# Two-block transformer, attention: ScalarE makes the new pair's exponentials before it copies the transposed pair

## What is computed

```python
s = jnp.einsum('bthd,btkd->bthk', qi, k_sel) * HEAD_DIM ** -0.5
p = masked_softmax(s, valid[:, :, None, :]).astype(v.dtype)
return jnp.einsum('bthk,btkd->bthd', p, v_sel)
```

```python
o = gi[..., 0:1] * o_c + gi[..., 1:2] * o_s + gi[..., 2:3] * o_w
```

```python
s = jnp.einsum('bshd,bnhd->bhsn', q, k).astype(jnp.float32) * HEAD_DIM ** -0.5
p = jax.nn.softmax(s, axis=-1).astype(v.dtype)
return jnp.einsum('bhsn,bnhd->bshd', p, v).reshape(B, S, MEM_Q)
```

## Time and profile before

| what | value |
|---|---|
| median of three runs | 3473.38 us |
| the profiled execution | 3475.57 us |
| its span (first to last instruction) | 3473.8 us |
| its mean granted TensorE clock | 0.966 |
| busy: PE, weight loads, VectorE, ScalarE, GpSimd | 94, 77, 46, 41, 46% of the span |

### The profile page before, as it was taken

How to read it: one execution, slowest core, us unless ns; L and a number is a source line. 1 busy time by engine, 2 the same in 40 slices (tenths; PEclk the granted TensorE clock), 3 DMA queues, 4 the chain that set the end, 5 groups by cost and what they waited for, 6 DMA issues and landing times.

```text
span 3473.8 us, 45512 instructions
## 1 busy us (share of the span) xinstructions
PE 3272.7 (94%) x16902; PEld 2669.8 (77%) x16902; DVE 1596.8 (46%) x2361; ACT 1438.5 (41%) x2575; POOL 1597.1 (46%) x1404
## 2 busy tenths in 40 slices
PE   6789999998999999999988996999999999999998
PEld 4567888876568888788877775888888888888886
DVE  4783443142743431444247875555565562234421
ACT  3355333223764333333235554454454532243332
POOL 4245445652555446444553321444444434464454
PEclk8899999997999999999999997999999999999999
DMA  4111333341013333333332120111111113333332
GB/s 121 45 43 55 97 97 95 94 116 37 1 32 96 96 95 95 91 97 95 96 82 60 51 61 25 31 38 42 38 37 37 41 46 99 98 95 97 97 96 68
DMA packets 471306, 245.86 MB, mean 71 GB/s; under 512 B 13819, under 2 KB 468710, under 8 KB 471014
## 3 DMA queue, kind: packets, MB, share of 16 engines
q1 hardware_dynamic: 470144, 241.33, 24.5%
q10 hardware_dynamic: 998, 2.30, 0.2%
HBM read 241.51 MB, written 2.10 MB: 70 GB/s over the span
## 4 chain that ended last, share of the span: by engine, by line
PE 84%; DVE 9%; ACT 4%; issue 2%; POOL 1%; DMA 0%; ACTq 0%; DVEq 0%; POOLq 0%
PE ps L464 18%; PE ps L466 18%; PE ps L465 18%; PE ps L2207 2%; PE ps L2311 2%; PE ps L2208 2%; PE ps L2209 2%; PE ps L1538 2%; PE ps L2293 2%; PE ps L1548 2%; PE ps L1561 1%; PE ps L1726 1%; PE ps L1799 1%; PE ps L1727 1%; PE ps L1728 1%
## 5 line engine op out<-in xcount | busy, mean ns | idle before, releaser
L446 POOL TENSOR_TENSOR w_lo<-ring,w_hi 128x512 fp32r<-128x512 f32 (+1 forms) x908 | 1222.7, 1368 | 1542.9 <-ACT w_hi L437 1542.9
L437 ACT ACTIVATE w_hi<-ring 128x512 fp32r<-128x512 f32 (+1 forms) x908 | 516.0, 617 | 1269.4 <-PE ps L466 1189.5
L464 PE MATMUL ps<-h_hi,w_hi 128*128 128x512 f32 x1776 | 702.7, 396 | 4.6 <-POOL w_lo L446 4.4
L466 PE MATMUL ps<-h_hi,w_lo 128*128 128x512 f32 x1776 | 693.4, 390 | 0.0
L465 PE MATMUL ps<-h_lo,w_hi 128*128 128x512 f32 x1640 | 640.1, 390 | 0.0
L464 PEld LDWEIGHTS ps<-h_hi,w_hi 128*128 128x128 f32 x1776 | 334.4, 188 | 81.1 <-POOL w_lo L446 6.4
L466 PEld LDWEIGHTS ps<-h_hi,w_lo 128*128 128x128 f32 x1776 | 334.1, 188 | 69.8
L465 PEld LDWEIGHTS ps<-h_lo,w_hi 128*128 128x128 f32 x1640 | 308.8, 188 | 68.2 <-issue 4.8
L465 PE MATMUL ps<-a_lo,w_hi 128*128 128x512 f32 x752 | 292.9, 390 | 0.0
L466 PE MATMUL ps<-a_hi,w_lo 128*128 128x512 f32 x720 | 280.4, 390 | 0.0
L464 PE MATMUL ps<-a_hi,w_hi 128*128 128x512 f32 x720 | 280.4, 389 | 0.0
(11 more groups left out here) (446 smaller groups left out, 5809.7 us busy)
## 6 DMA issues: line engine op xcount, KB each, us to landing
ring<-in_ffn_w_in SPq DMA_DIRECT2D x176, 512.0 KB, 3.8
ring<-in_w_in SPq DMA_DIRECT2D x96, 512.0 KB, 4.0
ring<-in_ffn_w_down SPq DMA_DIRECT2D x32, 512.0 KB, 4.1
ring<-in_ffn_w_out SPq DMA_DIRECT2D x32, 512.0 KB, 3.8
ring<-in_w_o SPq DMA_DIRECT2D x16, 512.0 KB, 4.1
ring<-in_w_branch_gdn SPq DMA_DIRECT2D x16, 512.0 KB, 3.8
ring<-in_nsa_w_in SPq DMA_DIRECT2D x15, 512.0 KB, 3.9
ring<-in_dsa_w_in SPq DMA_DIRECT2D x13, 512.0 KB, 4.1
```

What stands on the lines that cost most here:

```text
L437: act.activation(w_hi[:, (halves(u) + j) % PIECES, 0:n, :], slot(u)[:, j * n:(j + 1) * n, :], ACT.Copy) \
L446: pool.tensor_tensor(w_lo[:, q % PIECES, 0:n, :], slot(u)[:, j * n:(j + 1) * n, :], w_hi[:, q % PIECES, 0:n, :].bitcast(f32), ALU.subtract ...
L464: pe.matmul(dst, wh, hi(k), start=first and k == 0, stop=False)
L466: ins = pe.matmul(dst, wl, hi(k), start=False, stop=last and k == 2 * n - 1)
```

## The change

In each step of ScalarE's list the exponentials of step i now stand ahead of the copy of step i-3. The instructions, their operands and their semaphores are the same. (The two blocks are exchanged, so the exponentials are now on line 1624 and the copy on line 1634.)

```diff
         for i in range(S + LAG_V + 2):
-            s = i - LAG_T
-            if 0 <= s < S:
-                act.wait_ge(sig("att_turned").sem, t["turned"] + s + 1)
-                if s >= 2:
-                    act.wait_ge(sig("att_value").sem, t["value"] + s - 1)
-                w = min(P, us[2 * s]["nk"])
-                n_t = len(key_tiles(us[2 * s])) * P
-                act.activation(prT4[0:w, 2 * (s % 2):2 * (s % 2) + 2, 0:n_t], ps[0:w, 2:4, 0:n_t], ACT.Copy) \
-                   .then_inc(sig("att_copied").sem, 1)
             if i < S:
                 act.wait_ge(sig("att_max").sem, t["max"] + i + 1)
                 if i >= DEEP:
...
                 ins.then_inc(sig("att_prob").sem, 1)
+            s = i - LAG_T
+            if 0 <= s < S:
+                act.wait_ge(sig("att_turned").sem, t["turned"] + s + 1)
+                if s >= 2:
+                    act.wait_ge(sig("att_value").sem, t["value"] + s - 1)
+                w = min(P, us[2 * s]["nk"])
+                n_t = len(key_tiles(us[2 * s])) * P
+                act.activation(prT4[0:w, 2 * (s % 2):2 * (s % 2) + 2, 0:n_t], ps[0:w, 2:4, 0:n_t], ACT.Copy) \
+                   .then_inc(sig("att_copied").sem, 1)
             e = i - LAG_V - 1
             if pair_end(us, e):
```

## The result

The changed kernel took 3534.8 us, the median of four executions (3529.12 to 3547.99), the profiled one among them; the kernel before had 3473.52 us beside them (four runs, 3468.51 to 3478.00). The ratio is 1.0182, 95% interval 1.0154 to 1.0209: **slower by 61.3 us**. The forecast was 3521, with a range of 3497 to 3560. The profiled execution took 3531.99 us (span 3530.2), 56.4 us above the one before (3475.57). Its four runs (us, mean granted clock) are 3529.12 at 0.964, 3531.99 at 0.961, 3537.61 at 0.959 and 3547.99 at 0.956: the longer the run, the lower the clock.

The account below looks back on a forecast made before the run. The prediction took PE, a row of matmuls holding 84% of the chain of waits, as the bound. Its terms 10.4 + 24.8 + 12.6 = 47.8 us on the median 3473.38 gave 3521 us, range 3497 to 3560.

Parts of the forecast that it names:

- The bound, and what the change does: Both attention stages: PE nearly the bound; copy, transposes and values come behind the maximum, in the loop to scores two steps on.
- Layer 0, 4 x 2.59 = 10.4: Layer 0 attention: a pair takes 12.49 us instead of 9.90, over four full periods, 10.4 us more.
- Layer 1, 5 x 4.95 = 24.8: Layer 1 attention: a pair takes 28.3 us against 23.31, over the five pairs after the first, 24.8 us more.
- Half the sum of the operations, 26.9: Layer 1: lower bound for a pair, half of 53.8 us of operations for each of the even-step and odd-step loops.
- the walk: Layer 1: longest path through a pair's twelve steps, 2.2 + 6.3 + 5.2 + 1.7 + 5.8 + 7.1 = 28.3 us.
- The ends, 12.6: Both layers: memory-head steps 2.9 us, drain 1.2, passage into memory steps 0.4, fill 1.8; twice 6.3, bounds 5 and 16.
- GpSimd stays hidden: Attention stages: GpSimd's normalising comes out one step or more before the new copy, so it adds no time.
- The clock, costed at nothing: Attention stages: PE's layer 0 hole grows to about 2.4 us; holes this size went both ways, so 0 us charged.
- Partial cover: Both stages: loops bind only in the widest steps, PE's slack covers the rest; 24 us more, 3497 us; chance 0.13.
- Gain: Both stages: earlier exponentials start scores sooner and PE loses its waits; some 17 us less, 3456 us; chance 0.04.
- No effect: Both stages: ScalarE is no bound and PE's queue absorbs the change; 3473 us; chance 0.03.
- The clock rival: Both stages run partly at half clock: 23 us in layer 0, 15 in layer 1, 3559 us; chance 0.18.

Follow-up runs that it names:

- Experiment 2: Exponentials ahead of the copy only in layer 0's 512-key steps, or only its 128-key steps, against the kernel before: ratios 1.0058 (3492.59 us) and 1.0019 (3480.91 us).
- the first kernel of experiment 1: Exponentials ahead of the copy in layer 0 alone, old order in layer 1, against the kernel before: 3494.56 us, ratio 1.0062.
- the second kernel: Exponentials ahead of the copy in layer 1 alone, old order in layer 0, against the kernel before: 3516.62 us, ratio 1.0119.
- experiment 3: Exponentials ahead of the copy only in layer 1's narrow steps (31 keys), against the kernel before: 3476.46 us, ratio 0.9998.
- the per-head kernel of experiment 7: Old order on ScalarE, PE waits for each head's exponentials by itself, against the kernel before: 3473.56 us, ratio 0.9997.
- the filled kernel: The whole change plus three unread matmuls in steps 8 and 11 of each layer 1 pair after the first, against the kernel before: 3536.30 us, ratio 1.0168.

## Why the prediction was right, and where it was off

**The bound, and what the change does.** Right. PE is the bound, and the copy's place in ScalarE's queue put copy, transposes and values behind the maximum. The waits moved as forecast: ScalarE's before copies became waits for VectorE, and PE's own before L1548 for the copy went from 5.6 to 53.5 us in the whole program.

**Layer 0, 4 x 2.59 = 10.4.** Right: 4 x 2.47 = 9.9 at full clock. Experiment 2 takes the loop apart and finds its pieces.

**Layer 1, 5 x 4.95 = 24.8.** Right: 28.32 - 23.31 = 5.01, five times 25.0, and 24.3 with 28.17. (28.3 less 23.31 is 4.99; the 4.95 is a slip that costs 0.2 us.) Half the sum of the operations, 26.9, was too short. That the longest path passes from one loop to the other was argued, not shown, and the six terms of the walk name no rows, so only their total could be held against the runs; that it came so close may be luck in part, as taking the values out gave 26.33 us where some 25 was expected. In the twelve steps from 984.96 PE stands before L1548 for 0.39, 0.85, 1.31, 0.55, 1.58, 0.29 and 1.84 us.

**The ends, 12.6.** What is left of the 46.6 us when the pairs' 34.9 are taken off is 11.7. Near enough, though it holds whatever the clock took in the ends. Two pieces can be read apart. From the last 512-key scores to the end of the stage it was 24.13 us in layer 0 and 23.85 in layer 1 before, and at full clock with the new order 28.03 (the first kernel of experiment 1, from 275.72) and 28.28 (the second kernel, from 1030.95): 3.9 and 4.4 more, where 2.9 + 1.2 + 0.4 = 4.5 was forecast. From the first scores of layer 0 to the 512-key scores of its second pair it went from 16.68 to 18.56 us, 1.9 for the forecast's 1.8. Layer 1's fill has a clock of 0.51 before and 0.67 now, so what it added can't be told from the clock.

**GpSimd stays hidden.** Right. The largest of PE's weight-load waits is named after it (58.2 us), which looks like a new bound. The timeline of the full change, at a hole that has its name, shows what it is:

```profile
993.81 0.88 POOL L1649 TENSOR_SCALAR arena<-arena 128x128 f32<-128x128 f32 x2 [2.19 <-DVE arena L1604]
...
996.27 0.74 POOL L1649 TENSOR_SCALAR arena<-arena 128x31 f32<-128x31 f32 x2 [1.59 <-DVE arena L1604]
...
996.60 0.38 ACT L1634 ACTIVATE arena<-ps 128x256 f32<-128x256 f32 x1
...
997.12 0.41 PE L1548 MATMUL ps<-cst,arena 128*128 128x128 f32 x2 [1.31 <-POOL arena L1649]
```

The transposes at 997.12 are those of a 128-key step, and the normalising that they need is the one at 993.81, which ended at 994.69. The one that ended at 997.01 is of the narrow step behind it. What the transposes waited for is the copy, which ended at 996.98, 0.14 us before they start; the view names GpSimd because its last event came 0.03 us later. The hole before 257.26 in layer 0 is of the same kind: the wait of the weight load there is booked on GpSimd, PE's own row names the copy, and the pair's normalising had ended at 253.04.

**The clock, costed at nothing.** Here the forecast failed, and it is the mis-sized term: 10.9 us in the profiled execution (2.3 in layer 0, 8.6 in layer 1), which with the 47.8 of the sum comes to 58.7, against 57.5 measured in the stages. The hole itself was mis-sized too. The forecast had one of about 2.4 us from the end of the 128-key scores to the next transposes; there it is 1.14 us, and two more before transposes, of 1.45 (row 254.27) and 1.13, stand in the same pair, because the 128-key scores themselves stand behind the values that wait for the copy before. The earlier trace rows showed holes of this size going both ways, and the text chose the one that cost nothing and left the other at a chance of 0.18. They go both ways in the changed kernel as well, in the same program: windows 226:236, 236:246, 246:256 and 256:266 of the full change have 0.83, 0.99, 0.84 and 1.00. The right estimate was neither 0 nor the rival's 38: in layer 0 a fall ends within the pair, and 1.5 us more of PE's time (10.18 for 8.66) made the pairs only 0.35 to 1.23 us longer. The Trainium skill ("TensorE: Matmul & The Clock Gate", section "The HAM clock gate") had warned that the lower clock is the default and that activity releases it. The trace agrees in direction (0.89 to 0.96 in layer 1's pairs, where the kernel before had 1.00), and its rows show the two levels, 0.63 and 1.11 us for the same four transposes.

**The rivals.** Partial cover (24 us, 3497) fell: the pairs show the whole loops. Gain fell with experiment 3. No effect fell with the result. The clock rival was right in kind, in both layers, and its 38 us were 3.5 times too much for the profiled execution. In the second kernel of experiment 1 the clock took some 21 us of layer 1's stage (52.2 against 31), more than the 15 that the rival gave that layer.

**What stays open.** Why one execution loses the clock in a stretch in which another keeps it, and whether the fall would vanish if the thin stretch before it were filled. The runs show where it comes (behind the 256-key and narrow steps in the middle of a layer 1 pair, in three of four pairs of layer 0 in one profiled execution and in one or two of four in the others, and now and then in layer 1's old order), not what decides.

## What to carry to other kernels

In a software pipeline over engines with in-order queues, write down the loop of dependent work from one step to the step that reuses its result, and ask of every reordering what it puts behind the slowest link: a copy that was free in the shadow of VectorE's maximum cost its own time plus that of everything that PE had queued behind it. The idle time of an engine that is not the bound (41.1 us of ScalarE here) is no reserve: taking it away moved the waits to PE. When a change makes PE's work thinner, do not cost the clock at nothing: give it a term, between nothing and the full price. The runs may spread more as well (20 us in four runs of one program here, where the kernel before has some 10 to 15), but that is weak evidence: the per-head kernel of experiment 7, whose pairs are as before, also spread by 20 us.

## What the hardware showed that was not expected

- The granted clock falls at the same place of a pair, over and over, and comes back within the pair: in the filled kernel four pairs in a row are 30.73 to 30.75 us long, each with 0.89 over the whole and 0.72 in the same twelve microseconds.
- Shorter waits did not mean less time: with the copy between the heads, layer 1's loop should have been 2.6 us shorter, and its pairs had 0.78 in place of 0.89 to 0.96 and were as long as those of the full change or longer.
- The old order has falls too, but few. Beyond the first pair of layer 1, all 12 pairs of the three kernels with the new order there (the full change, layer 1 alone, the filled kernel) were below 1.00, and 3 of 24 in six kernels with the old one (PE busy for 21.6 to 22.4 of 23.3 us at full clock). How much PE is busy does not sort them by itself: in layer 0, one of four pairs fell where a pair has 8.64 us of work in 10.33, and others with 8.65 in 12.37 kept 1.00.
